# Two opening stages merged into one, gate columns moved to VectorE, squares summed per token block

## The chip, the core and the metric

The kernel runs on one core of one Trainium2 chip. The metric is the device time of one execution in microseconds (us). The core has TensorE (PE, matmuls), VectorE (DVE), ScalarE (ACT), GpSimd (POOL) and SyncE (SP), and 16 DMA engines. In this program SP, ACT and POOL also issue DMAs; in the profile these show as SPq, ACTq and POOLq.

## What is computed

Two transformer-like blocks run one after the other on 512 latent tokens of width 2048, the first with 256 context tokens beside them. Only the very beginning of the first block is touched here:

```python
mod = silu(c) @ w_ada + b_ada            # c: 2048, w_ada: 2048 x 6144; the same for c_ctx
shift, scale, gate = split(mod, 3)       # for latent tokens (c) and for context tokens (c_ctx)
u = rms_norm(h, pre_w) * (1 + scale) + shift       # 768 tokens x 2048
...                                      # u @ w_in, convolutions, two scans, output, block two
h_lat = h_lat + gate_l * merge(...)      # gate of the context tokens is not used at the end
```

`rms_norm(x, w)` is `x * rsqrt(mean(x*x) + eps) * w`. Besides, the opening brings small parameter vectors into columns, makes three small vectors for a later stage from `b_lambda_2` and `a_lb_logits_2`, and writes the latent tokens, feature-major, to scratch memory for the residual.

## The kernel before, in words

The program is a list of stages. Each is one block with an instruction stream per engine, and each ends with its semaphores cleared and a barrier of all engines; so no work of a stage starts before the last engine of the stage ahead is done. Within a stage each engine takes its stream in the written order, and waits are on semaphores.

Four stages matter here:

- `setup_stage`. SP loads five constant tables. ACT issues 22 small loads into `rows` (five tiles of 128x128), PE turns each tile (L1122) and DVE copies it to `cols` (L1129).
- `modulation_stage`. ACT loads six token tiles `tok` of 128 tokens (1 MB each, two buffers, L1218). PE turns each in four groups of four 128x128 blocks (L1198) and DVE copies each group to `x_all` (L1244), which is feature-major, 16 blocks x 768 tokens. ACT then issues the four stores of the latent tokens to `h_dram` (L1222) and only then makes `c_act`, the silu of c and c_ctx (L1225). Beside this SP loads `w_ada` in 12 groups of 512 columns (4 MB each, two buffers, L1185). For each group PE runs 16 fp32 matmuls with `c_act` (two columns) as the stationary operand and 512 columns moving (L1206; each fp32 matmul shows as two records), and DVE copies the 2x512 row out (L1270). At the end PE turns 48 pieces of the row into columns (L1210), and DVE adds the bias and makes gains and shifts (L1272 to L1278).
- `norm_stage("pre")`. ACT squares the 16 feature blocks (L1365), DVE and POOL add them up (L1338), PE sums over partitions with a matrix of ones (L1390, 4 fp32 matmuls), ACT turns that into the inverse root `inv` (L1369, L1372). Then the apply loop runs over 16 blocks: DVE multiplies by gain and `inv` (L1404), ACT adds the shift and rounds to a high part (L1379, L1383), DVE and POOL subtract for the low part (L1344).
- `project_stage("p1")` starts with two loads of a small weight on POOL (L1784) and four of `w_in` on SP (L1527).

The order is written out by hand. The line that starts the matrix work of the modulation is the wait for `c_act`; the two waits of a group are:

```python
pe.wait_ge(w_in[s], loads[s].value(it, 16))
pe.wait_ge(used.sem, used.value(it, s - 1))
```

## Time and profile before

| | us |
|---|---|
| median of 3 runs | 4553.44 (4553.36 to 4560.42) |
| profiled execution, its own time | 4547.87 |
| its span | 4546.1 |
| `setup_stage` | 0 to about 15.7 |
| `modulation_stage` | 15.7 to 235.0 |
| `norm_stage("pre")`, squares to `inv` | 235.9 to 263.0 |
| its apply loop | 263.1 to 303.7 |
| from there on, not touched | 303.7 to 4546.1 |

The times of stages are read from the timeline as starts of their first instruction on the queue or engine named in the rows further down. "[idle before <-X]" in a row is the time the engine stood still before it and what ended that. Records of PE are pipelined, so a group of them is read by its start and its length, not by a mean.

### The profile page before, as it was taken

What the parts mean: (1) busy time and instruction counts of PE and PEld (TensorE: products, weight loads), DVE (VectorE), ACT (ScalarE), POOL (GpSimd) and SP (SyncE); (2) the same over time, 40 slices, a digit from 0 to 9 for tenths busy, and PEclk for the clock granted to TensorE, in tenths of its full rate; (3) what the DMA queues carried; (4) which work ended last, traced back from release to release, by engine and by line L of the source; (5) the groups of instructions that cost most, each with busy time, mean ns of one, the idle gap of its engine ahead of it and who ended that gap; (6) DMA issues with size and microseconds to landing.
All of it is one profiled execution on the core that took longest, in us unless ns stands there. A gap on an engine that the chain in (4) does not pass through costs nothing. (4 is left out here: it accounts for less than half of the span.)

```text
span 4546.1 us, 53169 instructions
## 1 busy us (share of the span) xinstructions
PE 3797.5 (84%) x20530; PEld 3079.6 (68%) x20530; DVE 1872.7 (41%) x2775; ACT 1507.0 (33%) x2348; POOL 347.9 (8%) x257
## 2 busy tenths in 40 slices
PE   6939999997255665958999988878899999979696
PEld 2128888885254554847888867766689887868485
DVE  1043444431445444245455553243553344432344
ACT  0042222221244333225565552242422343431331
POOL 0020000000111034021010110001000000000000
PEclk9958999998578787979999999989999999989798
DMA  7702322242222102324222215132554454542131
GB/s 280 262 24 83 93 84 90 81 127 59 72 63 81 29 34 85 125 71 134 82 90 81 86 54 188 56 98 66 99 117 118 107 99 99 102 123 97 47 106 56
DMA packets 477416, 437.24 MB, mean 96 GB/s; under 512 B 56347, under 2 KB 415004, under 8 KB 475948
## 3 DMA queue, kind: packets, MB, share of 16 engines
q1 hardware_dynamic: 461472, 389.57, 30.7%
q10 hardware_dynamic: 11292, 27.81, 1.6%
q0 software_dynamic: 4464, 17.30, 1.1%
q8 instruction: 124, 2.03, 0.2%
q14 instruction: 64, 0.52, 0.0%
HBM read 379.22 MB, written 55.36 MB: 96 GB/s over the span
## 5 line engine op out<-in xcount | busy, mean ns | idle before, releaser
L1576 PE MATMUL o_acc<-y_in_hi,o_w_hi 128*128 128x512 f32 x768 | 301.9, 393 | 65.5 <-DVE o_w_lo L1698 65.5
L2154 DVE TENSOR_TENSOR od_w_lo<-od_w,od_w_hi 128x512 fp32r<-128x512 f32 x260 | 178.9, 698 | 402.9 <-ACT od_w_hi L2147 402.1
L2131 PE MATMUL od_acc<-od_u_hi,od_w_hi 128*128 128x512 f32 x784 | 318.5, 406 | 24.0 <-DVE od_u_lo L2260 19.1
L1576 PE MATMUL p_acc<-u_hi,p_w_hi 128*128 128x512 f32 x832 | 327.8, 394 | 2.8 <-DVE p_w_lo L1698 2.8
L1583 PE MATMUL p_acc<-u_hi,p_w_lo 128*128 128x512 f32 x832 | 328.1, 394 | 0.0
L1577 PE MATMUL p_acc<-u_lo,p_w_hi 128*128 128x512 f32 x832 | 324.4, 390 | 0.0
L2132 PE MATMUL od_acc<-od_u_lo,od_w_hi 128*128 128x512 f32 x784 | 312.1, 398 | 0.0
L2133 PE MATMUL od_acc<-od_u_hi,od_w_lo 128*128 128x512 f32 x784 | 311.7, 398 | 0.0
L1577 PE MATMUL o_acc<-y_in_lo,o_w_hi 128*128 128x512 f32 x768 | 301.2, 392 | 0.0
L1583 PE MATMUL o_acc<-y_in_hi,o_w_lo 128*128 128x512 f32 x768 | 301.1, 392 | 0.0
L2131 PE MATMUL ev_acc<-ev_u_hi,ev_w_hi 128*128 128x512 f32 x640 | 266.7, 417 | 39.0 <-DVE ev_u_lo L2260 38.1
L2147 ACT ACTIVATE od_w_hi<-od_w 128x512 fp32r<-128x512 f32 x260 | 161.1, 628 | 416.5 <-PE od_acc L2133 252.3
L1743 DVE TENSOR_TENSOR p_w_lo<-p_w,p_w_hi 128x1024 fp32r<-128x1024 f32 x100 | 121.9, 1225 | 392.8 <-ACT p_w_hi L1638 392.6
L2132 PE MATMUL ev_acc<-ev_u_lo,ev_w_hi 128*128 128x512 f32 x640 | 254.6, 398 | 0.0
L2133 PE MATMUL ev_acc<-ev_u_hi,ev_w_lo 128*128 128x512 f32 x640 | 254.4, 398 | 0.0
L1743 DVE TENSOR_TENSOR o_w_lo<-o_w,o_w_hi 128x1024 fp32r<-128x1024 f32 x84 | 102.8, 1226 | 309.6 <-ACT o_w_hi L1638 309.6
L1638 ACT ACTIVATE p_w_hi<-p_w 128x1024 fp32r<-128x1024 f32 x100 | 105.5, 1060 | 355.7 <-PE p_acc L1583 342.7
L2154 DVE TENSOR_TENSOR ev_w_lo<-ev_w,ev_w_hi 128x512 fp32r<-128x512 f32 x192 | 136.7, 739 | 204.9 <-ACT ev_w_hi L2147 204.5
L1576 PE MATMUL g_acc<-h_hi,g_w_hi 128*128 128x512 f32 x512 | 201.2, 393 | 18.7 <-DVE g_w_lo L1698 18.7
L1576 PEld LDWEIGHTS o_acc<-y_in_hi,o_w_hi 128*128 128x128 f32 x768 | 145.9, 190 | 97.9 <-DVE o_w_lo L1698 67.6
L1577 PE MATMUL g_acc<-h_lo,g_w_hi 128*128 128x512 f32 x512 | 200.9, 392 | 0.0
L1583 PE MATMUL g_acc<-h_hi,g_w_lo 128*128 128x512 f32 x512 | 200.8, 392 | 0.0
(543 smaller groups left out, 8457.9 us busy)
## 6 DMA issues: line engine op xcount, KB each, us to landing
od_w<-in_o_w_in_dram SPq DMA_DIRECT2D x260, 256.0 KB, 5.1
p_w<-in_w_in_dram SPq DMA_DIRECT2D x104, 512.0 KB, 3.8
mod_w<-in_w_ada_dram SPq DMA_DIRECT2D x12, 4096.0 KB, 13.6
ev_w<-in_e_w_in_dram SPq DMA_DIRECT2D x192, 256.0 KB, 2.9
g_w<-in_ple_gate_w_dram SPq DMA_DIRECT2D x64, 512.0 KB, 3.4
o_w<-in_w_out_dram SPq DMA_DIRECT2D x32, 512.0 KB, 3.6
o_w<-in_e_w_out_dram SPq DMA_DIRECT2D x32, 512.0 KB, 3.6
o_w<-in_o_w_out_dram SPq DMA_DIRECT2D x32, 512.0 KB, 3.4
```

What stands on the lines that cost most here:

```text
L1576: pe.matmul(lat, wh, x_hi[:, k, lat0:tokens], start=first, stop=False)
L1577: pe.matmul(lat, wh, x_lo[:, k, lat0:tokens], start=False, stop=False)
L1583: last = pe.matmul(lat, wl, x_hi[:, k, lat0:tokens], start=False, stop=end)
L1638: act.activation(w_hi[r][:], w[r][:], ACT.Copy).then_inc(hi_s, 1)
L1743: dve.tensor_tensor(w_lo[r][:], w[r][:], w_hi[r][:].bitcast(F32), ALU.subtract).then_inc(lo_s, 1)
L2131: pe.matmul(out, hi, self.x_hi[:, k, :], start=first, stop=False)
L2132: pe.matmul(out, hi, self.x_lo[:, k, :], start=False, stop=False)
L2133: last = pe.matmul(out, lo, self.x_hi[:, k, :], start=False, stop=end)
L2147: act.activation(self.w_hi[m % self.ring][:], self.w[m % self.ring][:], ACT.Copy).then_inc(self.hi_set, 1)
L2154: eng.tensor_tensor(self.w_lo[m % self.ring][:], self.w[m % self.ring][:], self.w_hi[m % self.ring][:].bitcast(F32), ALU.subtract).then_in ...
```

## The change

The two stages `setup_stage` and `modulation_stage` become one, `opening_stage`:

- PE and DVE turn the first four token tiles, then the first weight group; tiles 5 and 6 are turned after the first and the second group.
- The weight groups are now taken in the order both, both, gate, four times. "both" are the eight groups of shift and scale, done by PE as before. The four gate groups, needed for c alone, are done by DVE: one multiply and 15 multiply-adds of 128x512 along the feature axis that lies in the free dimension, then PE sums over partitions with ones (four one-column matmuls a group). There are three weight buffers instead of two.
- The rows are turned into columns group by group, after the next group's matmuls.
- ACT squares each token tile after it is copied, and DVE sums the 16 feature blocks of it with one reduction; PE sums over partitions after the fifth "both" group; ACT makes `x_inv` at the end of the stage.
- The small loads of constants and parameters move to POOL's queue; their turning into columns comes after the sixth "both" group.
- `c_act` is made after the second token load is issued.
- `norm_stage("pre")` gets `x_inv` and runs only its apply loop (`known=True`); SP stores the latent tokens to `h_dram` beside it (`keep`), in one DMA.

The diff, cut to its core:

```diff
 @stage
...
+def opening_stage(nc, a, consts, cols, mod, vec, x_all, x_inv):
...
     GROUP = 4
+    WIDE = GROUP * P
+    TILES = TOK // P
+    RING = 3
+    KINDS = ["both", "both", "gate"] * 4
...
         c_in, c_act = sb("c_in", 2, KD), sb("c_act", KD, 2)
-        w = [sb(f"w{i}", KD, GROUP * P) for i in range(2)]
+        w = [sb(f"w{i}", KD, WIDE) for i in range(RING)]
+        gate_acc, sq, sum_sq, eps = sb("gate_acc", 2, WIDE), sb("sq", KD, P), sb("sum_sq", TOK), sb("eps", 1)
...
+        def count(kind, n):
+
+            return sum(k == kind for k in KINDS[:n])
+
+        def column(n):
+
+            return (count("both", n) if KINDS[n] == "both" else 2 * KD // GROUP + count("gate", n)) * WIDE
+
+        def used(eng, n):
+
+            if KINDS[n] == "both":
+                eng.wait_ge(row_ready, count("both", n) + 1)
+            else:
+                eng.wait_ge(gate_sum, KD * (count("gate", n) + 1))
+
...
+            for n in range(len(KINDS)):
+                if n >= RING:
+                    used(sp, n - RING)
+                sp.dma_start(w[n % RING][:], w_v[:, :, column(n):column(n) + WIDE]).then_inc(w_in[n % RING], 16)
...
+            def both(n):
+                m = count("both", n)
+                pe.wait_ge(w_in[n % RING], 16 * (n // RING + 1))
+                if m >= 2:
+                    pe.wait_ge(row_set, m - 1)
+                for k in range(KD):
+                    last = pe.matmul(acc[m % 2][:, :], c_act[:, k, :], w[n % RING][:, k, :], start=(k == 0), stop=(k == KD - 1))
+                last.then_inc(row_ready, 1)
+
+            def row_out(m):
+                pe.wait_ge(row_set, m + 1)
+                for b in range(GROUP):
+                    last = pe.transpose(mod_p[:, m * GROUP + b, :], mod_row[:, m % 2, b * P:(b + 1) * P], ident[0:2, 0:2])
+                last.then_inc(row_turned, 1)
+
+            def gate(m):
+                pe.wait_ge(others_in, 16 * (len(consts) - 1))
+                pe.wait_ge(gate_sum, KD * (m + 1))
+                for b in range(GROUP):
+                    last = pe.matmul(mod_p[:, 2 * KD + m * GROUP + b, 0:1], gate_acc[:, m % 2, b * P:(b + 1) * P], ones[:, 0:1],
+                                     start=True, stop=True)
+                last.then_inc(gate_ready, 1)
+
+            for i in range(TILES - 2):
+                turn(i)
             pe.wait_ge(c_set, 1)
-            with pe.Fori(0, HALF) as it:
-                for s in range(2):
-                    pe.wait_ge(w_in[s], loads[s].value(it, 16))
-                    pe.wait_ge(used.sem, used.value(it, s - 1))
-                    for k in range(KD):
-                        last = pe.matmul(acc[s][:, :], c_act[:, k, :], w[s][:, k, :], start=(k == 0), stop=(k == KD - 1))
-                    last.then_inc(ready.sem, 1)
-            pe.wait_ge(used.sem, used.value(HALF, 0))
-            for b in range(MB):
-                last = pe.transpose(mod_p[:, b, :], mod_row[:, b * P:(b + 1) * P], ident[0:2, 0:2])
-            last.then_inc(turned, 1)
+            for n in range(len(KINDS)):
+                if KINDS[n] == "both":
+                    m = count("both", n)
+                    both(n)
+                    if m > 0:
+                        row_out(m - 1)
+                    if m < 2:
+                        turn(TILES - 2 + m)
+                    if m == 5:
+                        pe.wait_ge(rows_in, 16 * n_rows)
+                        for t in range(len(ROWS)):
+                            if t >= 4:
+                                pe.wait_ge(cols_set, 4)
+                            pe.transpose(cols_p[:, t % 4, :], rows[:, t, :], ident[:]).then_inc(cols_ready, 1)
+                    if m == 4:
+                        pe.wait_ge(others_in, 16 * (len(consts) - 1))
+                        pe.wait_ge(added, TILES)
+                        pe.matmul(wide[0][:].rearrange("p k t -> p (k t)"), ones[:], sum_sq[:, 0:512], start=True, stop=True)
+                        pe.matmul(wide[1][:].rearrange("p k t -> p (k t)")[:, 0:TOK - 512], ones[:], sum_sq[:, 512:TOK], start=True, stop=True
+                                  ).then_inc(sums_ready, 1)
+                elif n > 2:
+                    gate(count("gate", n) - 1)
+            gate(count("gate", len(KINDS)) - 1)
+            row_out(count("both", len(KINDS)) - 1)
 
...
+            def square(i):
+                act.wait_ge(copied, 4 * (i + 1))
+                if i > 0:
+                    act.wait_ge(added, i)
+                act.activation(sq[:], x_all[:, :, i * P:(i + 1) * P], ACT.Square).then_inc(sq_set, 1)
+
...
                 if i >= 2:
                     act.wait_ge(copied, 4 * (i - 1))
                 act.dma_start(tok[:, i % 2, :], a["ctx"][0, i * P:(i + 1) * P, :] if i < CTX_CHUNKS else
                               a["x"][0, (i - CTX_CHUNKS) * P:(i - CTX_CHUNKS + 1) * P, :]).then_inc(tok_in[i % 2], 16)
...
-            for g in range(4):
-                act.wait_ge(copied, 4 * TILES - 3 + g)
-                act.dma_start(h_dram[4 * g:4 * g + 4].rearrange("k p t -> p k t"),
-                              x_all[:, 4 * g:4 * g + 4, CTX:TOK]).then_inc(h_stored, 16)
-            act.wait_ge(c_loaded, 32)
-            act.activation(c_act[:].rearrange("p k w -> p w k"), c_in[:], ACT.Silu).then_inc(c_set, 1)
-
+                if i == 1:
+                    act.wait_ge(c_loaded, 32)
+                    act.activation(c_act[:].rearrange("p k w -> p w k"), c_in[:], ACT.Silu).then_inc(c_set, 1)
+                if i >= 2:
+                    square(i - 2)
             act.preload_act_table_set(EXP_LN)
+            for i in range(TILES - 2, TILES):
+                square(i)
+            act.wait_ge(cols_set, len(ROWS))
             act.activation(t0[:], columns(cols, "b_lambda_2"), ACT.Abs).then_inc(act_n, 1)
...
+            act.wait_ge(eps_set, 1)
+            for i, width in enumerate((512, TOK - 512)):
+                act.activation(x_inv[:, 512 * i:512 * i + width], wide[i][:].rearrange("p k t -> p (k t)")[:, 0:width], ACT.Ln,
+                               scale=1.0 / D, bias=eps[:, 0:1]).then_inc(ln_set, 1)
+            act.wait_ge(ln_set, 2)
+            act.activation(x_inv[:], x_inv[:], ACT.Exp, scale=-0.5).then_inc(inv_set, 1)
+
+        @block.gpsimd
+        def _(pool):
+            for key in consts:
+                if key != "ident":
+                    pool.dma_start(flat(consts[key][:]), a["c_" + key]).then_inc(others_in, 16)
+            pool.wait_ge(cleared, 1)
+            for t, tile in enumerate(ROWS):
+                at = 0
+                for key, n in tile:
+                    src = a[key]
+                    names = "abcdef"[:len(src.shape)]
+                    src = src if len(names) == 1 else src.rearrange(f"{' '.join(names)} -> ({' '.join(names)})")
+                    pool.dma_start(rows[at:at + n, t, :], src.rearrange("(r f) -> r f", f=P)).then_inc(rows_in, 16)
+                    at += n
+            pool.wait_ge(others_in, 16 * (len(consts) - 1))
 
...
+            def copies(i):
+                for g in range(4):
+                    dve.wait_ge(turned, 4 * i + g + 1)
+                    dve.tensor_copy(x_all[:, 4 * g:4 * g + 4, i * P:(i + 1) * P], wide[g][:]).then_inc(copied, 1)
+
+            def row(m):
+                dve.wait_ge(row_ready, m + 1)
+                if m >= 2:
+                    dve.wait_ge(row_turned, m - 1)
+                dve.tensor_copy(mod_row[:, m % 2, :], acc[m % 2][:, :]).then_inc(row_set, 1)
+
+            def gate(n):
+                m = count("gate", n)
+                total = gate_acc[:, m % 2, :]
+                dve.wait_ge(w_in[n % RING], 16 * (n // RING + 1))
+                dve.wait_ge(c_set, 1)
+                if m >= 2:
+                    dve.wait_ge(gate_ready, m - 1)
+                dve.tensor_scalar(total, w[n % RING][:, 0, :], c_act[:, 0, 0:1], None, ALU.mult).then_inc(gate_sum, 1)
+                for k in range(1, KD):
+                    dve.wait_ge(gate_sum, KD * m + k)
+                    dve.scalar_tensor_tensor(total, w[n % RING][:, k, :], c_act[:, k, 0:1], total, ALU.mult, ALU.add).then_inc(gate_sum, 1)
+
+            def lru():
+                l0, l1 = columns(cols, "a_lb_logits_2", 0, 8), columns(cols, "a_lb_logits_2", 8, 8)
+                dve.wait_ge(cols_set, len(ROWS))
+                link(dve.tensor_tensor(t1[:], l0, l1, ALU.max))
+                link(dve.tensor_tensor(t2[:], l1, t1[:], ALU.subtract))
+                link(dve.tensor_tensor(t1[:], l0, t1[:], ALU.subtract))
...
+            def sums(i):
+                dve.wait_ge(sq_set, i + 1)
+                dve.tensor_reduce(sum_sq[:, i * P:(i + 1) * P], sq[:].rearrange("p k t -> p t k"), AX.X, ALU.add).then_inc(added, 1)
+
+            for i in range(TILES - 2):
+                copies(i)
+                if i > 0:
+                    sums(i - 1)
+            row(0)
+            copies(4)
+            sums(3)
+            gate(2)
+            row(1)
+            copies(5)
+            sums(4)
+            row(2)
+            sums(5)
+            gate(5)
+            row(3)
+            row(4)
+            gate(8)
+            row(5)
+            for t in range(len(ROWS)):
+                dve.wait_ge(cols_ready, 4 if t < 4 else 5)
+                dve.tensor_copy(cols[:, t, :], cols_p[:, t % 4, :]).then_inc(cols_set, 1)
+            row(6)
+            lru()
+            gate(11)
+            row(7)
+            b_ada, pre = columns(cols, "b_ada"), columns(cols, "pre_norm_w")
+            dve.wait_ge(gate_ready, 4)
+            dve.wait_ge(row_turned, 8)
...
-
+            link(dve.tensor_tensor(mod[:, 2 * KD:MB, 0], mod_p[:, 2 * KD:MB, 0], columns(cols, "b_ada")[:, 2 * KD:MB], ALU.add))
...
-               feature_count=D):
+               feature_count=D, known=False, keep=None):
...
+        if keep is not None:
+            @block.sync
+            def _(sp):
+                sp.dma_start(keep[0].rearrange("b p t -> p b t"), keep[1]).then_inc(kept, 16)
+                sp.wait_ge(kept, 16)
...
-            act.preload_act_table_set(EXP_LN)
-            for k in range(K):
+            if not known:
+                act.preload_act_table_set(EXP_LN)
+            for k in range(0 if known else K):
...
+            if known:
+                return
             for i, (done, blocks) in enumerate(((dve_added, dve_sums), (pool_added, pool_sums))):
...
-            add_squares(dve, dve_sums, sum_sq[:, 0, :], dve_added)
-            dve.wait_ge(inv_set, 1)
+            if not known:
+                add_squares(dve, dve_sums, sum_sq[:, 0, :], dve_added)
+                dve.wait_ge(inv_set, 1)
...
-                setup_stage(nc, a, consts, cols)
...
+                        x_inv = inner.enter_context(nc.sbuf_tensor("x1_inv", [P, TOK], F32))
                         with nc.sbuf_tensor("mod", [P, 3 * KD, 2], F32) as mod:
-                            modulation_stage(nc, a, consts["ident"][:], cols, mod, vec, x_all, h_dram)
+                            opening_stage(nc, a, consts, cols, mod, vec, x_all, x_inv)
...
-                            (CTX, LAT, vec["gain_l"], vec["shift_l"])], parts=u)
+                            (CTX, LAT, vec["gain_l"], vec["shift_l"])], parts=u, inv=x_inv, known=True,
+                                   keep=(h_dram, x_all[:, :, CTX:TOK]))
```

## Rows read from the trace of the kernel before

**Rows 1.** The page's span and busy time of each engine over the whole run.
```profile
span 4546.1 us, 53169 instructions
PE 3797.5 (84%) x20530; PEld 3079.6 (68%) x20530; DVE 1872.7 (41%) x2775; ACT 1507.0 (33%) x2348; POOL 347.9 (8%) x257
```
**Rows 2.** Timeline, first 50 us: start, duration, engine, line, operation, out<-in; idle time before.
```profile
12.51 0.66 PE L1122 MATMUL set_cols<-k_ident,set_rows 128*128 128x128 f32 x2 [12.51 <-DMA set_rows<-in_c_conv_b_dram]
15.73 0.85 ACTq L1218 DMA_DIRECT2D mod_tok<-in_ctx_dram  x2
16.89 185.20 SPq L1185 DMA_DIRECT2D mod_w<-in_w_ada_dram  x12
...
20.72 6.29 PE L1198 MATMUL mod_turned<-k_ident,mod_tok 128*128 128x128 f32 x32 [6.04 <-DMA mod_tok<-in_ctx_dram]
32.93 5.32 PE L1198 MATMUL mod_turned<-k_ident,mod_tok 128*128 128x128 f32 x32 [5.92 <-DMA mod_tok<-in_x_dram]
```
**Rows 3.** The same view, TensorE alone, 36 to 330 us.
```profile
44.87 6.16 PE L1198 MATMUL mod_turned<-k_ident,mod_tok 128*128 128x128 f32 x32 [6.61 <-DMA mod_tok<-in_x_dram]
56.95 29.21 PE L1206 MATMUL mod_acc<-mod_w,mod_c_act 128*2 128x512 f32 x64 [5.92 <-ACT mod_c_act L1225]
87.15 27.63 PE L1206 MATMUL mod_acc<-mod_w,mod_c_act 128*2 128x512 f32 x64 [1.00 <-DMA mod_w<-in_w_ada_dram]
230.04 3.12 PE L1210 MATMUL mod_p<-k_ident,mod_row 2*128 2x2 f32 x48 [0.88 <-DVE mod_row L1270]
255.53 5.49 PE L1390 MATMUL pre_sums<-pre_sum_sq,k_ones 128*128 128x256 f32 x8 [22.37 <-DVE pre_sum_sq L1338]
```
**Rows 4.** The same view of VectorE, ScalarE and the queues, up to the projection.
```profile
233.20 0.26 DVE L1272 TENSOR_TENSOR mod<-mod_p,cols 128x96 f32<-128x96 f32 x1 [3.21 <-PE mod_p L1210]
235.96 0.06 DVE L1395 MEMSET pre_eps<- 128x1 f32 x1 [1.04 <-PEq L53]
263.08 2.21 DVE L1404 SCALAR_TENSOR_TENSOR pre_sq<-x,vec,pre_inv 128x256 f32<-128x256 f32 x4 [7.61 <-ACT pre_inv L1372]
303.68 2.98 SPq L1527 DMA_DIRECT2D p_w<-in_w_in_dram  x4
```
**Rows 5.** Windows: stretch, busy us (records) of PE, PEld, DVE, ACT, POOL, clock, DMA share, GB/s.
```profile
30.00:31.00 1.00, 0.00 (x0) 0.00 (x0) 0.00 (x0) 0.00 (x0) 0.00 (x0) 0.50 1.15 469
62.00:64.00 2.00, 2.00 (x6) 0.39 (x5) 0.00 (x0) 0.00 (x0) 0.00 (x0) 1.00 1.05 409
68.00:70.00 2.00, 2.00 (x6) 0.40 (x5) 0.00 (x0) 0.00 (x0) 0.00 (x0) 1.00 0.00 0
82.00:84.00 2.00, 2.00 (x6) 0.42 (x5) 0.00 (x0) 0.00 (x0) 0.00 (x0) 1.00 1.04 386
256.00:260.00 4.00, 4.00 (x8) 2.05 (x7) 0.00 (x0) 0.00 (x0) 0.00 (x0) 0.50 0.00 0
340.00:344.00 4.00, 4.00 (x20) 4.00 (x21) 0.00 (x0) 0.00 (x0) 0.00 (x0) 0.50 0.00 0
```
**Rows 6.** The page's list of DMA issues: count, KB each, median us to landing.
```profile
mod_w<-in_w_ada_dram SPq DMA_DIRECT2D x12, 4096.0 KB, 13.6
```
**Rows 7.** Instructions that price the vector work, by shape (busy, mean ns) and in the timeline.
```profile
L1244 DVE COPY x<-mod_turned 128x512 f32<-128x512 f32 x24 | 15.8, 688 | 21.2 <-PE mod_turned L1198 21.1
3308.31 2.32 DVE L2208 SCALAR_TENSOR_TENSOR od_mixed<-od_raw,cols,od_mixed 128x509 f32<-128x509 f32 x3
472.47 3.39 DVE L1728 SCALAR_TENSOR_TENSOR p_mixed<-p_raw,cols,p_mixed 128x496 f32<-128x496 f32 x4
L1404 DVE SCALAR_TENSOR_TENSOR pre_sq<-x,vec,pre_inv 128x512 f32<-128x512 f32 x16 | 18.1, 1130 | 0.0
L1695 DVE TENSOR_TENSOR y_in_lo<-o_x_ring,y_in_hi 128x2048 fp32r<-128x2048 f32 x12 | 27.5, 2292 | 57.9 <-ACT y_in_hi L1626 57.6
L935 ACT ACTIVATE ssd_y_sq<-ssd_y_g 128x2048 f32<-128x2048 f32 x2 | 3.8, 1910 | 14.5 <-DVE ssd_y_g L1025 14.5
```
**Rows 8.** One DMA issue group of GpSimd's queue, in the timeline.
```profile
303.91 2.46 POOL L1784 DMA_DIRECT2D p_w_small<-in_w_in_dram  x2 [2.68 <-POOLq L53]
```

145 lines of the change are left out of this document (45 added, 100 removed).

## The prediction

> **What bounds the kernel now.** I read the page's head first: over the run TensorE is busy 84% of 4546.1 us and nothing else passes 68% [rows 1]. That average says nothing about the opening, which is all that the change touches. So I read the timeline from the start to the first load of the projection, 303.68 us [rows 2 to 4], with three questions: who is late, is the DMA busy then, and which clock does TensorE have.
>
> The opening is a row of phases with one worker each. Up to 15.7 us the core waits for small loads and turns five tiles [rows 2]. From 15.73 us tokens come in; TensorE turns two tiles, then stands for 6 us until the next two land, twice [rows 2, 3]. The first weight matmul starts only at 56.95, released by ScalarE's `c_act`, which stands behind four stores on ScalarE's queue [rows 3]. Then TensorE is the bound: two groups take 27.63 us, with 1 us between pairs, to about 229 us [rows 3]. In that stretch the DMA works in bursts: 386 to 409 GB/s, then nothing, as at 68 to 70 us [rows 5]. At 230 us come 3.12 us of turning the row and the small vector steps; the norm stage opens at 235.96 [rows 3, 4]. From there to 263.08 nothing but squares, sums and the inverse root happens; its matmuls end at 261.02 [rows 3, 4]. The apply loop then takes 263.08 to 303.68, 40.6 us, and has VectorE as its bound [rows 4].
>
> **The change, part by part.** Times "after" are from the start of the new span.
>
> 1. First loads. `setup_stage` vanishes as a phase. The first token load goes out at about 1.0 instead of 15.73, so the token rows move by 14.7: tiles 1 and 2 are turned from 6.0 to 12.3, tiles 3 and 4 from 18.2 to 23.5 [rows 2]. VectorE's reduction of tile 2 stands between their copies. The trace has no reduction. Its nearest row is a vector operation over 128x2048 at 2.29 us; as bounds I take ScalarE's 1.91 over as many elements below, and twice the row, 4.6, above, since the reduction reads with a stride. I take 2.3, so the four tiles end at 26 [rows 7]. ScalarE's square of a tile is 1.91 us [rows 7] and lies beside.
>
> 2. The DMA stream. One weight load is 4096 KB = 4.19 MB [rows 6]; 12 of them, 6.29 MB of tokens and 0.8 MB of small loads are 57.4 MB. With several loads queued the trace shows 409 GB/s, in the weight phase 386 [rows 5]. A load takes 13.6 us to landing, of which 10.9 are bytes at 386, so 2.7 is latency that a queued load hides [rows 6]. I take 409 for the token phase (13.4 MB, 32.8 us) and 386 for the 44.0 MB behind it (114.0 us): the last group lands at 1.0 + 2.7 + 146.8 = 150.5, the others 10.9 apart before it: groups 0 to 8 (counting from 0) at about 26, 42, 53, 64, 74, 85, 96, 107, 118, and groups 9 and 10 at 129 and 140. All at 409 gives 144. All twelve one by one at 13.6 gives 182, which is a rival below.
>
> 3. Does the stream ever run dry? SP issues load n+3 when group n is used. A "both" group is 13.8 us of TensorE. A gate group is one multiply and 15 chained multiply-adds; three chained ones of nearly that size take 2.32 us, so 0.785 from start to start, and another chain of four shows 0.887 (3.39 us) [rows 7]. I take 0.785, since its form (row of 509, wait on the one before) is the nearer: 0.5 + 15 x 0.785 = 12.3 us, with 13.8 at the other value and 17.5 at the 1.13 us that the same operation takes with POOL beside it [rows 7]. POOL has no arithmetic in the new stage. TensorE: both(0) 26 to 41.5, tile 5, both(1) to 58.3, tile 6, both(2) 64 to 78, both(3) to 92, both(4) 96 to 110, the sums of squares, both(5) 112 to 126. VectorE: gate(2) 53 to 65, gate(5) 85 to 98, gate(8) 118 to 130.5. So load 3 is issued at 42, when load 2 is still 11 us from landing, load 4 at 58 (6 before load 3 lands), load 8 at 98, load 9 at 110, load 10 at 126 (3 before load 9 lands), load 11 at 130.5. The stream stays full, with the least reserve at loads 4 and 10.
>
> 4. What each added wait holds up. VectorE takes gate(8) and row(5) before it copies `cols`; TensorE's fifth turn waits for these copies, and both(6) is queued behind it. 130.5 + 0.7 (row) + 1.4 (four copies) + 0.5 gives 133.2, though group 9 landed at 129 and TensorE was free at 126. TensorE has then stood for some 7 us. After gaps of 6 us its clock was at 0.50, the lower level of 1.2 GHz [rows 2, 5], and the first pair of groups after such a gap took 29.21 instead of 27.63 [rows 3]. So both(6) is 15.4 us, to 148.6; row(6) to 149.3; `lru()`, ten tiny operations and one exchange with ScalarE, 2.6 us, to 151.9. Only then gate(11) starts, though its load landed at 150.5: to 164.2. both(7) ends at 162.5 beside it.
>
> The Trainium skill (TensorE: Matmul & The Clock Gate, section HAM oscillation) says of this that a wait between bursts of matmuls lets the clock gate close, and that the next burst starts slow each time. The trace agrees: 0.50 at 30 us, in the gap [rows 5]. By that rule the gap before both(4) would also cost 1.6 us; the sum would not move, since load 7 is queued until 107.
>
> 5. The end. row(7), four turns and four one-column sums: 1.1, to 165.3; 9 vector operations at 0.21: 1.9, to 167.2; stage change 1.1, as from about 234.9 to the first multiply that could follow 235.96 [rows 4]. The apply loop starts at 168.4 instead of 263.08: **94.7 us earlier**.
>
> 6. The norm stage loses squares, sums and inverse root. Added is one 4.19 MB store on SP, 13.6 us against a loop of 40.6; it is costed at nothing, and if it were uncovered it would cost up to 13.6 [rows 4, 6]. Vector copies of 0.69 us ran beside a full DMA before [rows 7], so I don't expect the loop to stretch. Squares and sums of tiles in the opening are 6 x 2.3 us on VectorE, all before gate(5), where it waits for loads anyway. `x_inv` is ready by about 152.
>
> 7. The small loads on POOL: two issues take 2.46 us [rows 8], 26 take 32 us. TensorE asks for them at 126. The cover is 90 us.
>
> **How the sum stands to the runs.** Span 4546.1 - 94.7 = 4451.4. Around the span lie 1.8 us (4547.87 - 4546.1), and the median of the runs is 5.6 above the profiled execution. Against the median: 4553.4 - 94.7 = **4458.7**.
>
> **Rivals.**
>
> A. The stream is not gapless: loads pay their 13.6 us one by one. For it: a single load alone shows that number [rows 6]. Against: 409 GB/s while several were queued [rows 5]. Last landing 182, apply loop at 199, gain 64: 4489. A half way (gaps at loads 4, 10, or 13.8 for a gate) gives gains of 75 to 88. Together 0.17.
>
> B. More than the sum: 409 GB/s throughout and no cold start. The last load lands at 144, but gate(8) and the copies still hold both(6) to 128, gate(11) runs 145.5 to 157.8, loop at 162: gain 101, 4452. With the quieter runs of the profiled kind 4447. Chance 0.08.
>
> C. The end on the other side: TensorE stays at 1.2 GHz through the opening, because it waits so often. The sums of squares ran at 0.50: 3072 columns in 5.49 us, two records per fp32 matmul [rows 3, 5]; a "both" group of 16384 record columns is then 29 us, and with DMA waits hidden at least 27.5. 26 + 8 x 27.5 + two tiles, sums and turns (18) + 5 gives 269, the loop at 269: 6 us later than now, 4559. If the clock then stays low into the projection, as it does now at 340 us with TensorE fully busy [rows 5], every 10 us there costs 5 more, and past 10 us it is over 0.2%. It decides from about 27 us a group; below that something is gained. Against it: by 62 us, 5 us after the start at 56.95, the clock was at 1.00, and at 82 it still was, [rows 3, 5]. Chance 0.04, half of it past 0.2%.
>
> D. The parameter loads come late on POOL. The Trainium skill (DMA: Bandwidth & Descriptors, section SWDGE vs HWDGE vs iDMA) says that GpSimd writes its descriptors to a part of SBUF from which VectorE's two-port mode locks it out. No run here shows it. In this kernel it would act while VectorE copies or multiplies from SBUF with one source, which the opening hardly does. Nothing is lost until an issue costs 4.9 us (126 / 26) instead of 1.23 [rows 8]; at 8.6 us the gain is gone. Chance 0.03, at about 4500.
>
> E. The forecast, gains of 88 to 101: 0.68.
>
> **How the numbers follow.** The time is that of E. The range leaves out C, D and the slower half of A: a gain of 77 on the high side, 4476; on the low side B with the profiled execution's offset and some spread, 4445. It holds 0.8. About 0.2% (9 us) can be told from no change here. Faster by more: 0.96 (A, B, D, E); within: 0.02 (half of C); slower: 0.02 (the other half).
>
> **What would show it.** Right: the loop's first multiply near 168; weight loads 10.9 us apart with a DMA share near 1 from 4 to 150; a stand of TensorE of 7 us before both(6), released by VectorE's copy of `cols`; gate(11) as the last long piece, 12 us, behind `lru()`; no idle over 1 us in the loop; all after the projection's start as before. Wrong: landings over 12 us apart (A), the clock at 0.50 in "both" groups beyond the first 4 us (C), TensorE waiting for a parameter load (D), or a reduction of 4 us and more.

## The result, and the profile of the changed kernel

The changed kernel takes **4476.57 us** (median of its runs, 4472.40 to 4477.81) against 4556.93 for the kernel before, timed beside it: a ratio of 0.9825, 95% interval 0.9813 to 0.9836. The gain is 80.4 us. I had forecast 94.7 and a time of 4458.7; the time lies 0.6 us above the upper end of my range. 3.5 us of the distance are the reference itself: I had counted from 4553.4, the median of the three runs that I had.

The head of the page of the changed kernel, as [rows 1] of before:

```profile
span 4476.0 us, 52848 instructions
PE 3749.2 (84%) x20414; PEld 3074.6 (69%) x20414; DVE 1921.0 (43%) x2833; ACT 1504.9 (34%) x2337; POOL 351.2 (8%) x279
```

The timeline of TensorE in the opening (start, duration, engine, line, operation, out<-in, idle time before and what ended it), as [rows 2, 3]:

```profile
19.05 5.58 PE L1176 MATMUL mod_wide<-k_ident,mod_tok 128*128 128x128 f32 x32 [7.07 <-DMA mod_tok<-in_x_dram]
27.73 13.89 PE L1185 MATMUL mod_acc<-mod_w,mod_c_act 128*2 128x512 f32 x32 [3.10 <-DMA mod_w<-in_w_ada_dram]
...
44.95 13.89 PE L1185 MATMUL mod_acc<-mod_w,mod_c_act 128*2 128x512 f32 x32 [1.43 <-DMA mod_w<-in_w_ada_dram]
...
66.63 15.90 PE L1185 MATMUL mod_acc<-mod_w,mod_c_act 128*2 128x512 f32 x32 [5.56 <-DMA mod_w<-in_w_ada_dram]
...
135.09 0.48 PE L1218 MATMUL mod_cols_p<-k_ident,mod_rows 128*128 128x128 f32 x1 [5.60 <-DVE cols L1358]
...
137.00 16.55 PE L1185 MATMUL mod_acc<-mod_w,mod_c_act 128*2 128x512 f32 x32
```

The same view of VectorE, as [rows 4]; the last row is the start of the apply loop:

```profile
29.29 3.63 DVE L1336 TENSOR_REDUCE mod_sum_sq<-mod_sq 128x128 f32<-128x2048 f32 x1
...
121.36 0.49 DVE L1314 TENSOR_SCALAR mod_gate_acc<-mod_w,mod_c_act 128x512 f32<-128x512 f32 x1 [7.72 <-DMA mod_w<-in_w_ada_dram]
121.88 11.78 DVE L1317 SCALAR_TENSOR_TENSOR mod_gate_acc<-mod_w,mod_c_act,mod_gate_acc 128x512 f32<-128x512 f32 x15
...
156.65 0.49 DVE L1314 TENSOR_SCALAR mod_gate_acc<-mod_w,mod_c_act 128x512 f32<-128x512 f32 x1
157.17 11.78 DVE L1317 SCALAR_TENSOR_TENSOR mod_gate_acc<-mod_w,mod_c_act,mod_gate_acc 128x512 f32<-128x512 f32 x15
168.86 0.67 DVE L1305 COPY mod_row<-mod_acc 2x512 f32<-2x512 f32 x1
...
173.64 2.21 DVE L1509 SCALAR_TENSOR_TENSOR pre_sq<-x,vec,x_inv 128x256 f32<-128x256 f32 x4
```

Windows (stretch, busy us and records of PE, PEld, DVE, ACT, POOL, granted clock, DMA share, GB/s), as [rows 5]:

```profile
8.00:12.00 4.00, 3.72 (x26) 3.25 (x24) 3.55 (x7) 1.25 (x2) 4.00 (x9) 1.00 1.04 356
12.00:16.00 4.00, 0.00 (x0) 0.00 (x0) 4.00 (x3) 0.90 (x1) 2.55 (x6) 1.00 1.06 355
64.00:68.00 4.00, 1.37 (x2) 0.21 (x3) 3.82 (x7) 0.00 (x0) 0.00 (x0) 0.50 1.04 387
82.00:96.00 14.00, 14.00 (x37) 2.96 (x36) 11.60 (x13) 0.00 (x0) 0.00 (x0) 1.00 1.04 385
96.00:100.00 4.00, 2.98 (x17) 1.54 (x16) 3.82 (x6) 0.00 (x0) 0.00 (x0) 1.00 0.61 193
132.00:136.00 4.00, 0.91 (x5) 0.91 (x5) 3.26 (x9) 0.07 (x1) 0.00 (x0) 0.52 1.04 389
152.00:156.00 4.00, 4.00 (x14) 0.96 (x13) 1.77 (x8) 1.02 (x4) 0.00 (x0) 1.00 0.24 87
```

The loop starts at 173.64 instead of 263.08, 89.4 us earlier; my sum said 94.7. Yet the span is only 70.1 us shorter, and the medians 80.4. The rest was given back far behind the opening, where both programs have the same instructions: in the odd block. I measure its **stretch** from the first `od_bank` matmul to the first square of the final norm. First the two rows of before, then the two of after:

```profile
3208.73 1.02 PE L2285 MATMUL od_bank<-od_sum_sq,k_ones 128*128 128x512 f32 x2
4499.20 0.61 ACT L1365 ACTIVATE fn_sq<-h 128x512 f32<-128x512 f32 x1
```

```profile
3126.04 1.02 PE L2391 MATMUL od_bank<-od_sum_sq,k_ones 128*128 128x512 f32 x2
4428.11 0.61 ACT L1466 ACTIVATE fn_sq<-h 128x512 f32<-128x512 f32 x1
```

Before 1290.5 us, after 1302.1. TensorE's own work in it did not grow. The same view as the windows above, over the stretch: before, after, and two kernels of the experiments below, h2 and f1:

```profile
3208.73:4499.20 1290.47, 1197.94 (x6147) 1009.04 (x6145) 515.26 (x685) 419.00 (x604) 38.09 (x24) 0.96 0.43 98
3126.04:4428.11 1302.07, 1198.86 (x6147) 1010.12 (x6145) 515.24 (x685) 418.91 (x605) 38.06 (x24) 0.96 0.43 97
3233.42:4533.02 1299.60, 1197.98 (x6147) 1008.86 (x6145) 515.33 (x685) 419.15 (x605) 38.05 (x24) 0.96 0.42 98
3215.30:4524.26 1308.96, 1197.40 (x6147) 1009.71 (x6145) 515.18 (x685) 419.17 (x604) 38.08 (x24) 0.96 0.45 97
```

TensorE is busy 1197.9 us before and 1198.9 after, so 10.7 of the 11.6 us are time in which it stands idle. The page's list of DMA issues (count, KB each, median us to landing) shows the odd block's weight loads landing later. Before, then after:

```profile
od_w<-in_o_w_in_dram SPq DMA_DIRECT2D x260, 256.0 KB, 5.1
```

```profile
od_w<-in_o_w_in_dram SPq DMA_DIRECT2D x260, 256.0 KB, 5.8
```

The list of waits (us in total, times, longest) shows two places that wait for loads: ScalarE for weights, and TensorE for `od_v_tok`, which is no weight but an intermediate result read back from scratch memory. Before (3160 to 4070 us), then after (3070 to 3995):

```profile
ACT od_w_hi L2147 <- DMA od_w<-in_o_w_in_dram: 20.2, 10, 3.5
PE od_bank L2918 <- DMA od_v_tok<-s_v: 13.7, 3, 7.0
```

```profile
ACT od_w_hi L2253 <- DMA od_w<-in_o_w_in_dram: 32.0, 10, 5.1
PE od_bank L3024 <- DMA od_v_tok<-s_v: 21.3, 3, 9.9
```

These windows open some 50 us ahead of the stretch. Inside the stretch the first wait is 12.3 us before and 18.7 after, six times in both. So the two waits grow by 6.4 and 7.6 us there; some of that overlaps, and the stretch grows by 11.6.

### The profile page after: what moved, and what is told of

Same layout as the page of the kernel before. It is cut to its first block and busy times, and to the rows that moved or that the text cites. A ratio compares the mean times of both kernels' runs of the same rounds, so it can differ in the third digit from the quotient of the medians.

```text
span 4476.0 us, 52848 instructions
## 1 busy us (share of the span) xinstructions
PE 3749.2 (84%) x20414; PEld 3074.6 (69%) x20414; DVE 1921.0 (43%) x2833; ACT 1504.9 (34%) x2337; POOL 351.2 (8%) x279
## 5 line engine op out<-in xcount | busy, mean ns | idle before, releaser
L1744 ACT ACTIVATE o_w_hi<-o_w 128x1024 fp32r<-128x1024 f32 x84 | 89.1, 1060 | 337.1 <-PE o_acc L1689 327.9
```

The costliest lines, as they stand in the source:

```text
L1744: act.activation(w_hi[r][:], w[r][:], ACT.Copy).then_inc(hi_s, 1)
```

## The experiments

Three questions: is the loss in the odd block real, what did each part of the opening do, and what makes identical instructions slower. "The stretch" is read from the same two rows in each run.

### Is it real: both kernels again

Neither has an edit. Theory V: the difference of the stretch is variation from run to run. Theory L: it belongs to the change.

> The kernel before, unchanged, for a second trace. In the traces at hand the changed kernel reaches the projection 89.1 us earlier but ends only 70.1 us earlier; the missing 19.0 us are lost between the odd block's projection and the end, where ScalarE waits 32.0 instead of 20.2 us for loads of od_w. Theory L (lost by the change: something the opening leaves behind slows the loads of the odd block): the stretch from the projection's first load to the end is again 4242 us (4240 to 4245) here, with 20 us of waits for od_w. Theory V (it varies from execution to execution, and the profiled execution of before was a quick one, 5.6 to 9 us under its own median): this stretch comes out anywhere from 4242 to 4262, most likely near 4250, with the waits for od_w moving with it.

> The changed kernel, unchanged, second trace and more rounds. Theory L: the stretch from the projection's first load to the end is 4261 us again (4259 to 4264). Theory V: between 4245 and 4262, and the ratio to the kernel before stays at 0.981 to 0.984 because both vary alike. Both: the opening repeats to 1 us, apply loop at 173 to 174.

Measured: 4556.92 with a stretch of 1289.5, and 4477.08 (ratio 0.9828, 0.9814 to 0.9841) with 1302.5 and the loop at 173.1. Between these two spans, 4548.7 and 4471.5, the projection's first load is 90.4 us earlier and the end 77.2; 13.0 of the missing 13.2 are in the stretch. Theory L holds. The first pair of profiles had lost a further 6.4 us between the projection's first load and the stretch; this pair does not, so that was variation. Over all profiles of this document that part lasts 2905 to 2921 us, whatever the length of the program (f2, as long as the kernel before, has 2918). It goes with the granted clock: TensorE was at 0.50 for 593 to 614 us of it in the six shortest and for 618 to 631 us in the five longest. A single span is therefore a poor measure of the loss, and the stretch a better one.

### The opening: gate groups back on TensorE

```
-    KINDS = ["both", "both", "gate"] * 4
+    KINDS = ["both"] * 12
```

> The opening as one program, but the four gate groups back on TensorE (twelve groups of one kind, rows evicted by VectorE, three buffers kept). Theory of the prediction (TensorE's groups at 13.8 us are the next bound, so moving a third of them off is what brings the opening from there to the DMA stream): groups back to back from 27.7 us: 12 x 13.9 + 9 for tiles, turns and sums, apply loop near 207; 33 us slower than the changed kernel, 47 us faster than before. Rival (the loads bound it anyway, at 10.9 us a group, and the place of the gate group hardly matters): apply loop at 175 to 180, within 6 us of the changed kernel.

Measured: 4517.28 (0.992, 0.9904 to 0.9935), 40.2 us slower than the changed kernel. The groups stand back to back on TensorE:

```profile
177.05 13.90 PE L1185 MATMUL mod_acc<-mod_w,mod_c_act 128*2 128x512 f32 x32
191.21 13.89 PE L1185 MATMUL mod_acc<-mod_w,mod_c_act 128*2 128x512 f32 x32
...
209.41 1.15 DVE L1504 SCALAR_TENSOR_TENSOR pre_sq<-x,vec,x_inv 128x256 f32<-128x256 f32 x2
```

So of the 89.4 us that the loop moved, 35.8 (209.41 to 173.64) are the gate groups on VectorE. By difference the other 54 are the merged opening and the squares that left the norm stage; no run separates those two.

### The opening: parameter copies and `lru()` earlier

```
-                    if m == 5:
+                    if m == 4:
                         pe.wait_ge(rows_in, 16 * n_rows)
...
+            for t in range(len(ROWS)):
...
+            lru()
             gate(8)
             row(5)
-            for t in range(len(ROWS)):
...
             row(6)
-            lru()
```

> The turning of the parameter rows and the small vectors moved ahead of gate(8), into a stretch where VectorE waits 7.7 us for a load. Theory: in the changed kernel the copies of cols stand behind gate(8), hold TensorE for 5.6 us and leave it at the lower clock (both(6) 16.5 instead of 13.9 us), so gate(11) starts 3.5 us after its load. Without that: both(6) starts near 131 and takes 13.9, gate(11) starts with its load at 152 to 153, apply loop at 169 to 170, 4 us earlier, 4 us off the time. Rival (the last load and the chain behind it set the end alone, the hold is hidden): apply loop stays at 173 to 174.

Measured: 4480.46 (0.9834, 0.9821 to 0.9848), the loop at 174.27; the theory had said 169 to 170. TensorE no longer waits 5.6 us for `cols`, and both(6) has the full clock from its start. But both(5) ends 2.8 us later than in the changed kernel: 1.7 of that come from the turns ahead of it, and 1.1 from both(4), which the edit does not touch and which ran partly at the low clock (0.50, that is 1.2 GHz) in this execution. So load 10 is issued later, and the stream goes dry; gate(11) then waits for its load. The windows, then rows of the timeline:

```profile
128.00:132.00 4.00, 4.00 (x16) 1.20 (x14) 3.82 (x6) 0.00 (x0) 0.00 (x0) 1.00 0.46 170
132.00:136.00 4.00, 4.00 (x15) 1.28 (x15) 1.03 (x2) 0.00 (x0) 0.00 (x0) 1.00 0.81 263
```

```profile
98.42 15.59 PE L1185 MATMUL mod_acc<-mod_w,mod_c_act 128*2 128x512 f32 x32 [1.77 <-DMA mod_w<-in_w_ada_dram]
...
132.62 13.89 PE L1185 MATMUL mod_acc<-mod_w,mod_c_act 128*2 128x512 f32 x32
...
156.28 0.49 DVE L1314 TENSOR_SCALAR mod_gate_acc<-mod_w,mod_c_act 128x512 f32<-128x512 f32 x1 [9.05 <-DMA mod_w<-in_w_ada_dram]
```

In the changed kernel that load landed at 154.8 and gate(11) started at 156.65 behind `lru()`; here it starts at 156.28, as its load lands. So the load alone would have let gate(11) start at most 1.9 us earlier, and the edit made the load 1.5 us later.

### The opening: squares stored so that the reduction reads in order

```
-    sq [KD, P];  act.activation(sq, ...);  tensor_reduce(..., sq.rearrange("p k t -> p t k"))
+    sq [P, KD];  act.activation(sq.rearrange("p t k -> p k t"), ...);  tensor_reduce(..., sq)
```

> The squares of a token tile are stored with the feature block as the innermost index, so that VectorE's reduction reads them one after the other; ScalarE writes with the stride instead. Measures the term that was taken from another operation: the reduction of 128x2048 took 3.6 us against 2.3 supposed. Theory S (the stride costs the 1.3 us): the reduction falls to 2.2 to 2.4 us; both(0) starts 1 to 2 us earlier, the apply loop 0 to 2 us earlier. Rival (the operation itself is slow): it stays at 3.5 to 3.7 us, and nothing moves. In both the time is within 3 us of the changed kernel.

Measured: 4476.09 (0.9826, 0.9811 to 0.9842), the loop at 171.81, and this reduction:

```profile
44.39 2.26 DVE L1336 TENSOR_REDUCE mod_sum_sq<-mod_sq 128x128 f32<-128x2048 f32 x1
```

It takes 2.26 us in place of 3.62, so the stride alone costs 1.36 us. The loop comes 1.3 to 1.8 us earlier. The time can't show that much. The profiled execution was the slowest of the four (4481.58), with a stretch of 1308.9. The Trainium skill (SBUF — State Buffer, section Door 1: The DMA port swizzle) says that SBUF is read by lines of 16 bytes and that each step onto a new line costs. The stride here was 512 bytes, and the run agrees in direction: 1.6 times the duration.

### The stretch: order of first use, and queues

Theory P: tensors in DRAM are placed by the order in which the program first names them. Theory Q: what ran on which queue in the opening leaves the queues in another state. The first edit restores the old order of naming, the second the old queues:

```
 e6:  GpSimd's part written first, and k_ident loaded there
 e7:  constants on SyncE, 22 parameter loads and four h stores on ScalarE, none on GpSimd
```

> The changed kernel with only this moved: the identity matrix is loaded on POOL's queue too, and POOL's stream is written ahead of SP's, so that the tensors in HBM are named for the first time in exactly the order of the kernel before. Everything after the opening is the same instructions at the same on-chip addresses in all kernels, yet the stretch from the first od_bank matmul to the final norm took 1290.7 and 1289.7 us before, and 1302.3, 1302.7, 1306.4, 1301.8 in four traces with the new opening. Theory P (the order of first use decides where tensors lie in HBM, and with that how fast the odd block's weights load): 1290 (1289 to 1292) here, 12 us off the time, 4465. Theory Q (what was issued earlier on SP's and ACT's DMA queues leaves them in another position): 1302 to 1306, time 4477.

> The changed kernel with its DMAs on the queues of the kernel before: constants on SP, the 22 parameter loads and the four stores of latent tokens on ACT's queue, none on POOL's. The tensors are then first named in another order than before. Theory Q (position of the queues): the stretch from the first od_bank matmul to the final norm falls to 1290. Theory P (place in HBM by order of first use): it stays at 1302 or takes a third value. Opening: apply loop at 173 to 176.

Measured: 4477.07 (0.9825, 0.9808 to 0.9843) with a stretch of 1300.6, and 4477.32 (0.9836, 0.982 to 0.9852) with 1302.4. Both theories fall in this form. The four stores on ScalarE made the loop 43.6 us long instead of 40.9.

### A faster opening

The edit moves the turns of the parameter rows behind both(1) and both(2), `lru()` ahead of gate(8) and the sums of squares behind both(6), and splits the last weight load into four pieces.

> Towards a faster kernel: the parameter rows turned before both(2) and both(3), where TensorE and VectorE wait for loads; the small vectors ahead of gate(8); the sums of squares after both(6) instead of before both(5); the last gate group's load in four pieces, so that its chain starts on the first. Theory (both the load stream and the chain after the last load set the end; e4 freed only the middle and made both(5), and with it load 10, 2.7 us later): no dry stretch of the stream after 100 us, gate(11) ends 3 to 4 us after its last piece instead of 12 to 16, TensorE's both(7) ends last near 160, apply loop at 164 to 166, 8 to 10 us earlier: 4467 to 4469. Rival (the pieces load slower than one big load, or the order frees nothing): apply loop at 171 or later.

Measured: 4474.08 (0.9825, 0.9812 to 0.9838), the loop at 169.20, with a stretch of 1302.7. The theory had said 164 to 166 and its rival 171 or later; neither came out. The loop is 4.4 us earlier than in the profiled changed kernel. The time is 3.0 us below the changed kernel's 4477.08, which is less than a measurement here can tell. both(6) still starts at the low clock, now behind its load:

```profile
132.08 15.72 PE L1190 MATMUL mod_acc<-mod_w,mod_c_act 128*2 128x512 f32 x32 [4.11 <-DMA mod_w<-in_w_ada_dram]
```

### The stretch: one property at a time, from the kernel before

Theory S: the written-out program. Theory T: how early the odd block comes. Theory N: the moved store of `h`.

```
 f1:  -  with pe.Fori(0, HALF) as it:      +  for it in range(HALF):     (SyncE and VectorE too)
 f2:  -  HALF = MB // GROUP // 2           +  HALF = MB // GROUP // 4    (rows of the first half stand in)
 f3:  -  four act.dma_start(h_dram[...])   +  one sp.dma_start(keep[0], keep[1]) in the norm stage
```

> The kernel before, with its three modulation loops (SyncE, TensorE, VectorE) written out as straight instructions; nothing else. It asks why the stretch from the first od_bank matmul to the final norm lasts 1302 to 1309 us in every kernel with the new opening and 1290 us in the kernel before. Theory S (the length of the program and where its instructions lie): the stretch becomes 1300 or more here too, and the time some 12 us longer than before, 4565 to 4570. Theory T (how long after the start the stretch comes): 1290 and 4555 to 4560, since the opening takes as long as before. Theory N (something that the new stages leave behind, h store or norm): 1290 too.

> The kernel before with its modulation loop run three times instead of six: the second half of w_ada is not loaded or multiplied, and the rows of the first half stand in for it (the output is not the reference's). The program is as long as before; everything behind the modulation starts some 100 us earlier (six groups of 17.3 us). Theory T (how long after the start the odd block comes): the stretch from the first od_bank matmul to the final norm becomes 1300 us or more, and the time 4465 to 4470. Theory S (length of the program) and theory N (the new stages): the stretch stays 1290 and the time is 4452 to 4456.

> The kernel before with one part of the change alone: h is stored by one DMA of SyncE in the norm stage rather than by four of ScalarE in the modulation. Theory N (the moved store leaves later loads in another state): the stretch from the first od_bank matmul to the final norm becomes 1300 us or more. Theories S and T: it stays 1290. The time otherwise within 3 us of the kernel before, since the store lies beside the norm loop of 40 us.

Measured: f1 4572.68 (1.0036, 1.0022 to 1.005) with a stretch of **1309.0**; f2, which loads and multiplies only half of `w_ada`, 4470.16 (0.981, 0.9794 to 0.9826), loop at 177.2, stretch 1290.4; f3 4545.43 (0.9983, 0.9973 to 0.9993), stretch 1291.2. T and N fall. (The time of f2 is no evidence for T: the loop came 85.9 us earlier and not the 100 that I had expected, and the stretch stayed.) S is shown for this much: written-out loops, in an otherwise old kernel, are enough to slow the odd block by 18.5 us. The rows of f1:

```profile
3215.30 1.02 PE L2285 MATMUL od_bank<-od_sum_sq,k_ones 128*128 128x512 f32 x2
4524.26 0.61 ACT L1365 ACTIVATE fn_sq<-h 128x512 f32<-128x512 f32 x1
```

And its line of waits (3160 to 4080 us), 20.2 us before:

```profile
ACT od_w_hi L2147 <- DMA od_w<-in_o_w_in_dram: 32.9, 11, 4.9
```

f3 is 8.8 us faster than the kernel before; I had expected under 3. Without the four stores ahead of `c_act` on ScalarE's queue the loop starts at 256.4, about 7 us earlier.

### The stretch: filler that does no work

The compiled program of TensorE is 2,057,408 bytes before, 2,083,008 in the changed kernel and 2,098,368 in f1. The page counts its loading:

```profile
q8 instruction: 124, 2.03, 0.2%
```

That is the page of before (queue and kind: packets, MB, share). 124 packets and 2.03 MB are 16 KB each. Theory F: a place in these blocks decides when each is loaded. Theory M: only the length matters. Theory O: something else of the new stages. The filler is a wait that is met already, repeated:

```
+            for _ in range(288):          # g1; 224 in g2 and g3, 512 in h2
+                pe.wait_ge(ident_in, 16)
```

> The kernel before with 288 waits on TensorE that are met already, behind the first wait of the setup, where TensorE is idle; no work changes. They make TensorE's compiled program 9,216 bytes longer, so that its end lies at the same place of a 16 KB block as in the changed kernel (0.137 of a block, against 0.574 before). Theory F (the place of TensorE's instructions in the blocks that the instruction queue loads decides when each block is loaded, and with what that collides): the stretch from the first od_bank matmul to the final norm becomes 1300 us or more, and the time 4565 or more. Theory O (only what the new stages or written-out loops leave behind matters, not the place): the stretch stays 1290 and the time 4553 to 4560.

> The changed kernel with 224 waits on TensorE that are met already, ahead of the first token tile, where TensorE is idle; no work changes. They bring the end of TensorE's program to the place of the kernel before (0.574 of a block). Theory F: the stretch from the first od_bank matmul to the final norm returns to 1290 us, and the time to 4463 to 4467. Theory O: the stretch stays 1302 and the time 4474 to 4479.

> The same filler in the reordered opening of e8_best. Theory F: 4460 to 4464 with a stretch of 1290 us. Theory O: 4472 to 4476 with 1303 us.

Measured: g1 4565.34 (1.0021, 1.0012 to 1.003), stretch 1298.4; g2 4479.23 (0.9832, 0.9819 to 0.9845), 1302.7; g3 4480.62 (0.9836, 0.9823 to 0.9849), 1308.6. In the profile of g1 the stretch is 8 us longer, but that execution was the slowest of ten (4574.7). The median of g1 is 8.9 us above the kernel before, and its loop starts 7 us later, so the medians leave only some 2 us behind the opening. g1 alone proves little. Restoring the place gives the new kernel nothing.

> The changed kernel with waits that are met already on TensorE, ScalarE, VectorE and SyncE, each where its engine is idle in the opening, in such numbers that the program of each engine ends at the same place of a 16 KB block (TensorE) or of an 8 KB block (the others) as in the kernel before. Theory F (the place of the instructions in the blocks that are loaded, on all engines together): the stretch from the first od_bank matmul to the final norm returns to 1290 us, and the time to 4463 to 4468. Theory M (the length of the program, and with it where other things lie in memory) and theory O (something else of the new opening): 1302 us and 4474 to 4480.

> The kernel before with 512 met waits on TensorE in the setup: its program becomes longer by exactly one block of 16 KB, so that every later instruction has the same place in its block. The setup becomes some 10 us longer, since TensorE is idle there only until the rows have landed. Theory F: the stretch from the first od_bank matmul to the final norm stays at 1290 us. Theory M: it becomes 1298 us or more, as with the filler of 9,216 bytes.

> As h1, in the reordered opening of e8_best. Theory F: 4460 to 4465 with a stretch of 1290 us. Theories M and O: 4472 to 4478 with 1303 us.

Measured: h1 4480.99 (0.9837, 0.9823 to 0.985), 1304.4; h2 4582.98 (1.006, 1.0044 to 1.0075), 1299.6; h3 4476.59 (0.9826, 0.9813 to 0.9839), 1305.2. h1 restores the place on every engine and gains nothing; h2 keeps every place and its stretch is 9 us longer. Theory F falls on both sides. The time of h2 also holds a loop that starts 17.5 us later, as its filler stands on the path. Its median is 26.2 us above the kernel before, so 9 us are left behind the opening here too. The lines of waits of h2 (3178 to 4093 us):

```profile
ACT od_w_hi L2149 <- DMA od_w<-in_o_w_in_dram: 28.3, 9, 5.0
PE od_bank L2920 <- DMA od_v_tok<-s_v: 19.7, 4, 9.2
```

Both are longer than before (20.2 and 13.7), though the weight loads land in 5.2 us in the median, against 5.1.

### The stretch: the new opening with loops

```
+            with pe.Fori(0, 3) as it:     # six token tiles, two a pass
+                turn(0, it); turn(1, it)
...
+            with pe.Fori(0, 3) as it:     # the last six matmul groups, two a pass
+                both(3, it); (sums of squares); both(4, it)
```

> The reordered opening of e8_best with TensorE's part as loops: the six token tiles by a loop of three passes over two tiles, all of them ahead of the first group, and the last six matmul groups by a loop of three passes over two groups (the sums of squares are made in each pass and used after the third); what turns the rows comes behind it. TensorE's program is 2,058,624 bytes long, 1,216 more than before and 24,384 less than in the changed kernel. Since both(0) waits for the sixth tile (some 43 us instead of 28), the stream of loads stops for some 5 to 10 us, and the norm loop starts at 170 to 178 us. Theory M (the length of TensorE's program): the stretch from the first od_bank matmul to the final norm returns to 1290 to 1292 us, and the time is 4464 to 4473. Theory O (something else of the new opening, which runs here too): the stretch stays 1302 us or more, and the time is 4476 to 4485.

Measured: 4481.25 (0.9831, 0.9817 to 0.9844), the loop at 178.5, stretch 1299.2. TensorE's program is only 1,216 bytes longer than before, and the stretch is 3 us shorter than in the changed kernel but still 9 longer than before. Both theories had given another number.

The stretch against the length of TensorE's program, all runs:

| kernels | bytes more than before | stretch, us |
|---|---|---|
| before, e1, f2 | 0 | 1290.5, 1289.5, 1290.4 |
| f3 | 64 | 1291.2 |
| i1 (new opening) | 1,216 | 1299.2 |
| g1 | 9,216 | 1298.4 |
| h2 | 16,384 | 1299.6 |
| after, e2, e4, e5, e6, e7, e8 | 25,472 to 25,600 | 1302.1, 1302.5, 1301.5, 1308.9, 1300.6, 1302.4, 1302.7 |
| g2, g3, h1, h3 | 32,768 | 1302.7, 1308.6, 1304.4, 1305.2 |
| e3, f1 | 39,936, 40,960 | 1306.2, 1309.0 |

Up to 64 bytes more the stretch is 1289.5 to 1291.2 us, in every other kernel 1298.4 and more. Among kernels of one length single profiles lie some 8 us apart, so a finer order than that is not shown, and 1,216 bytes go with as much as 16,384. The medians agree in the main: the time against the kernel before, less what the projection's first load moved, is 20 us for f1, 15 for e3, 14 for e8, 11 for e2, 9 for h2 and i1, but 2 for g1 and for f2. With old stages alone h2 shows that met waits on TensorE are enough, and f1 that written-out loops are.

**What stays open** is how the instructions of the opening reach the waits for loads 2900 us later: whether by where things come to lie in memory or by something else. Longer landing times are a part of it at most: in h2 the waits grow with nearly the median landing time of before. No run here looks at addresses.

The Trainium skill (Runtime: NRT & Kernel Launch, section Instruction fetch mechanics) says that instructions are loaded by blocks of 16 KiB with 256 instructions, that passing into the next block is mostly hidden, and that kernels prefer full unrolling where possible, because a taken branch may wait for its block. The block size agrees with the rows of q8. The advice does not pay here: the loops of the kernel before, written out, start the loop 1.4 us earlier (261.7 against 263.1) and cost 18.5 us in the odd block.

## Why the prediction was off

**Step 1, first loads: right in the sum, a term too small.** The tiles ended at 24.6 (26 forecast) and both(0) started at 27.73, when its load had landed. The reduction takes 3.6 us, not 2.3; it was inside my bounds, and I had taken the row nearest in size while the stride pulled towards the upper one.

**Step 2, the stream: the term of 409 GB/s for the token phase was too high.** From 3 to 45 us the DMA moved 387 GB/s in the mean, and only 355 from 8 to 16 us, at a share of 1.04 and more. At 387 instead of 409 the 15.5 MB up to load 1 take 2.2 us longer, by my estimate; load 1 landed at 44.9 instead of 42, and with this every later load was 2.9 us late. From load 1 to load 8 the forecast holds: 76.4 us against 76, one load each 10.8 us but for load 7. The last load landed at 154.8 instead of 150.5.

**Step 3, "the stream stays full": wrong, but cheap.** Load 3 landed at 66.6 instead of 64. TensorE had stood for 5.56 us, so both(2) started at the low clock (15.90 us, clock 0.50), for which I had no term, and ended at 82.5 instead of 78. Through both(3) this delayed the issue of load 7, and from 96 to 100 the DMA moved 193 GB/s: load 7 landed 11.5 us after load 6, which is 0.7 lost. Load 10, one of the two that I had named as those with the least reserve, landed 11.8 us after load 9, another 1.0. Load 8 landed at 121.3 instead of 118, and 2.9 of these 3.3 us are those of step 2. The gate group itself was right: 0.49 + 11.78 = 12.3 us. For the gap before both(4) the prediction gave a possible price of 1.6 us; the gap was 1.02 us long, and the group took 13.89.

**Step 4, the wait for `cols`: right, with its cost.** TensorE waited 5.60 us for VectorE's copies (some 7 forecast), the granted clock was 0.52 in the mean of 132 to 136, and both(6) took 16.55 us (15.4 forecast). Its start slipped by 3.8 us, from load 8, and its length by 1.1. gate(11) ran 156.65 to 168.9 behind `lru()` as described, 4.7 us late.

**Step 5, the end: 0.6 short.** From the end of gate(11) 4.8 us to the loop, not 4.2. So 5.2 us in all: 3.8 + 1.1 + 0.6, less 0.3 in the small pieces between. Loop at 173.6 against 168.4.

**Step 6, the norm stage: right.** The store of `h` is hidden; the loop takes 40.9 us (40.6 before). In e7, with the stores on ScalarE, the loop takes 43.6.

**Step 7, the small loads: right in the result.** 26 issues were through at 14.55 us, 0.5 each, against 1.23 that I took from [rows 8].

**"All after the projection's start as before": wrong, and the larger part of the miss.** The odd block, 2900 us later, lost 12 to 13 us with unchanged instructions. I had put it at nothing without a reason but that its instructions stay the same. No rival named it either. Rival A gave a gain of 75 to 88 for a half-dry stream, and the 80.4 falls into it; that is luck, since the gaps in the stream cost under 2 us. Luck too is that the gain lies above the 77 from which I drew the upper end of my range: the margin was meant for the stream, and the odd block used it up.

In numbers, from the pair e1 and e2: their spans differ by 77.2 us, 17.5 less than 94.7. Of these, 4.3 are lost before the projection's first load and 13.0 in the stretch. The medians of the first measurement differ by 80.4, some 3 more than these two spans; both profiled executions of the kernel before were quick ones (4547.87 and 4550.48 against medians of 4553 to 4557), so the medians put the loss behind the opening at 9 to 11 us. Against the forecast of 4458.7 the time is 17.9 too high: 14.3 for the smaller gain and 3.5 for the reference.

## What to carry to other kernels

Where a ring of loads feeds two engines, moving one small piece of work shifts a load's issue, so an edit must be followed through to the next loads: e4 removed a stall of 5.6 us and gained nothing. A rate read in one window of 2 us need not hold for long: 409 GB/s was read from such a window [rows 5], 387 came over 42 us, and the delay stayed to the end. A gain made early in a long kernel should be checked by the length of later stages and not by the total alone: the first and last instruction of an untouched stage, two rows per kernel, found this loss. And writing loops out is not free even where it saves time on the spot; in f1 it was paid for in a stage that has nothing to do with it.

## What the runs showed of the hardware

- An untouched stage of 1290 us took 8 to 18 us more when instructions ahead of it were changed (1299.6 in h2 with met waits on TensorE alone, 1309.0 in f1). TensorE's busy time in it stayed at 1197 to 1199 us; its idle time grew from 92.5 us to 101.6 and 111.6.
- Identical loads of that stage took 5.1 us to landing in the median before, 5.8 after and 6.2 in f1, but 5.2 in h2.
- A reduction over 128x2048 fp32 takes 2.26 us when it reads in order and 3.62 with a stride of 512 bytes.
- GpSimd issued 26 small loads at about 0.5 us each; two larger ones in [rows 8] had taken 1.23.
- A group of 16 fp32 matmuls of 128x512 after a gap of 5 to 6 us took 15.90 and 16.55 us, with a clock of 0.50 to 0.52 in the gap; one that follows the one before without a gap took 13.89. Between the two the length of the gap did not decide: 13.89 after 3.10 us in the changed kernel, 15.59 after 1.77 us in e4.
